# Expert activations turned by VectorE in blocks of 32x32 instead of by TensorE, in a one-layer SSD + GLA + MoE step

## The reference

```
def moe_ffn(h, comb, wg, wu, wd):
    out = jnp.zeros_like(h)
    for e in range(N_EXPERTS):                       # 16
        ye = (jax.nn.silu(h @ wg[e]) * (h @ wu[e])) @ wd[e]
        out = out + comb[:, e:e + 1].astype(h.dtype) * ye
    return out
```

## Time and profile before

| | before |
|---|---|
| median of 3 runs | 1048.48 us |
| profiled execution, its time | 1046.16 us |
| its span, first to last instruction | 1044.0 us |
| TensorE busy | 994.8 us (95%) |
| VectorE busy | 386.0 us (37%) |
| ScalarE busy | 232.8 us (22%) |
| read from memory, written | 212.31 MB, 24.36 MB |

### The profile page before, as it was taken

The page is one execution under the profiler, slowest core; times in us unless marked ns, Lnnn a source line. Parts: engine busy times, 40 slices in busy tenths (PEclk is TensorE's granted clock), DMA queues, the critical chain, the costliest instruction groups (busy, mean ns, idle before and its releaser), DMA issues.

```text
span 1044.0 us, 20310 instructions
## 1 busy us (share of the span) xinstructions
PE 994.8 (95%) x8547; PEld 750.8 (72%) x8547; DVE 386.0 (37%) x850; ACT 232.8 (22%) x466; POOL 138.0 (13%) x228
## 2 busy tenths in 40 slices
PE   4999999999989899999999999997889999999996
PEld 2667676676766566666666767665789999999981
DVE  3121235667435986656641611225110101101016
ACT  2131222323352222242251300002320101111013
POOL 0000232352000252422400000000100000000010
PEclk9999999999999899999999999999889999999998
DMA  9853346456453456655533633432739999999993
GB/s 381 317 197 121 122 161 207 157 211 220 148 195 119 177 184 214 219 208 196 175 140 121 251 121 121 161 106 82 291 140 349 408 406 405 392 398 412 391 355 122
DMA packets 47155, 237.62 MB, mean 228 GB/s; under 512 B 6800, under 2 KB 11248, under 8 KB 23792
## 3 DMA queue, kind: packets, MB, share of 16 engines
q1 hardware_dynamic: 45120, 230.85, 59.2%
q0 software_dynamic: 1520, 5.34, 1.5%
q10 hardware_dynamic: 448, 0.50, 0.1%
HBM read 212.31 MB, written 24.36 MB: 227 GB/s over the span
## 4 chain that ended last, share of the span: by engine, by line
PE 87%; DVE 4%; ACT 3%; issue 2%; DMA 1%; POOL 1%; ACTq 0%; DVEq 0%; SPq 0%; POOLq 0%
PE pjB L827 15%; PE pjA L827 14%; PE states L1370 11%; PE pjA L1218 7%; PE pjB L1218 7%; PE states L1373 6%; PE pjB L1370 3%; PE pjA L1370 3%; PE pjA L1373 1%; PE pjB L1373 1%; PE states L836 1%; PE bank L1182 1%; PE states L1197 1%; PE bank L951 1%; PE states L951 1%
## 5 line engine op out<-in xcount | busy, mean ns | idle before, releaser
L827 PE MATMUL pjB<-hF,ring 128*128 128x320 f32 x608 | 174.1, 440 | 0.0
L827 PE MATMUL pjA<-hF,ring 128*128 128x320 f32 x608 | 171.9, 436 | 0.5 <-ACT regA L1616 0.5
L1373 PE MATMUL states<-ring,oF 128*32 128x384 f32 x1392 | 155.3, 493 | 0.0
L1370 PE MATMUL states<-ring,oF 128*32 128x128 f32 x1392 | 155.3, 273 | 0.0
L1370 PEld LDWEIGHTS states<-ring,oF 128*32 128x32 f32 x1392 | 152.5, 110 | 0.6 <-issue 0.3
L827 PEld LDWEIGHTS pjB<-hF,ring 128*128 128x128 f32 x608 | 114.8, 192 | 49.7 <-issue 6.3
L827 PEld LDWEIGHTS pjA<-hF,ring 128*128 128x128 f32 x608 | 113.2, 190 | 50.7 <-issue 7.0
L2605 DVE TENSOR_TENSOR oF<-oF,states 128x384 f32<-128x384 f32 x15 | 8.3, 554 | 153.5 <-PE states L1373 153.5
L2337 DVE TENSOR_TENSOR G<-G 128x320 f32<-128x320 f32 x32 | 46.6, 1494 | 0.0
L1954 POOL TENSOR_TENSOR G<-regA,G 128x128 f32<-128x128 f32 (+1 forms) x32 | 18.9, 592 | 195.1 <-ACT G L1672 195.1
L1373 PE MATMUL pjB<-ring,hF 128*32 128x384 f32 x360 | 42.2, 493 | 0.0
(11 more groups left out here) (504 smaller groups left out, 1431.6 us busy)
## 6 DMA issues: line engine op xcount, KB each, us to landing
ring<-in_w SPq DMA_DIRECT2D x171, 1024.0 KB, 8.1
G<-in_ss SPq DMA_DIRECT2D x16, 512.0 KB, 4.0
out_ss_new<-G SPq DMA_DIRECT2D x16, 512.0 KB, 2.7
G<-csd SPq DMA_DIRECT2D x16, 320.0 KB, 3.5
G<-in_sg SPq DMA_DIRECT2D x4, 1024.0 KB, 6.2
out_sg_new<-G SPq DMA_DIRECT2D x16, 256.0 KB, 2.8
yd<-hF SPq DMA_DIRECT2D x14, 288.0 KB, 6.2
rF<-in_w SPq DMA_DIRECT2D x2, 1024.0 KB, 9.1
```

The costliest lines, as they stand in the source:

```text
L827: mm = pe.matmul(pj[g % 2][:, 0:T], w[:, k, half * P:half * P + P], hF[:, k, :], start=(k == 0), stop=(k == KT - 1))
L1370: pe.matmul(bank[CAP:P, c * P:(c + 1) * P], rows(c, True), w[:, WIDE:512], start=first and c == 0, stop=last, tile_position=(0, CAP), skip ...
L1373: mm = pe.matmul(bank[QUAD * c:QUAD * c + QUAD, 0:WIDE], rows(c, False), w[:, 0:WIDE], start=first, stop=last, tile_position=(0, QUAD * c) ...
```

## The change

All transposes but those of expert 15 leave TensorE. VectorE turns `actE` itself with 16 instructions per expert: each takes a block of 32 partitions (token block `c`) with three pieces of 32 columns, transposes the pieces, and writes them to partition group `q` of `actT`. The copy from bank 4 goes, except for expert 15 (`turned_last`). The wait for `s_rd` before `actE` is written again becomes a wait for `s_hev`, which VectorE's own last block counts.

```
             def down(e, back, turn=None):
...
                     mm.then_inc(s_used, 1)
-                    if turn and h == 0:
-                        turn_act(turn[0])
...
                     if isinstance(e, int) and e == 0:
                         for t in range(1, XROWS // P):
                             turn_tokens(t)
-                        turn_act(0)
...
                 def turned(e, v):
 
-                    dve.wait_ge(s_rd, GH + PAIRS + 1 + e)
+                    dve.wait_ge(s_eac, e + 1)
                     if not (isinstance(e, int) and e < 2):
                         moe_used(dve, e, 5, 2)
+                    for q in range(4):
+                        to = slice(QUAD * q, QUAD * q + QUAD)
+                        for c in range(4):
+                            at = slice(QUAD * c, QUAD * c + QUAD)
+                            rows = slice(QUAD * c, QUAD * c + QUAD) if c < BLOCKS else slice(CAP, P)
+                            ins = dve.transpose(actT[to, v, :, rows],
+                                                actE[at, :].rearrange("p (k f) -> p k f", f=P)[:, :, QUAD * q:QUAD * q + QUAD])
+                    ins.then_inc(s_hev, 1)
+
+                def turned_last(v):
+
+                    dve.wait_ge(s_rd, GH + PAIRS + 1)
+                    moe_used(dve, E - 1, 5, 2)
                     dve.tensor_copy(actT[:, v], b[4][:, 0:WIDE].rearrange("p (k c) -> p k c", k=BLOCKS)).then_inc(s_hev, 1)
```

In one() and last() the wait before `actE` changes in the same way:

```
-                        dve.wait_ge(s_rd, GH + PAIRS + e)
+                        dve.wait_ge(s_hev, XROWS // P + e)
```

More of the change, by code:

```diff
@@ L2617, in last @@
                     dve.wait_ge(s_esg, e + 1)
-                    dve.wait_ge(s_rd, GH + PAIRS + e)
+                    dve.wait_ge(s_hev, XROWS // P + e)
                     dve.tensor_tensor(actE, sgE, b[3][:, 0:WIDE], ALU.mult).then_inc(s_eac, 1)
-                    turned(e, v)
+                    turned_last(v)
                 def turned(e, v):
-                    dve.wait_ge(s_rd, GH + PAIRS + 1 + e)
+                    dve.wait_ge(s_eac, e + 1)
                     if not (isinstance(e, int) and e < 2):
                         moe_used(dve, e, 5, 2)
+                    for q in range(4):
[9 more added lines that the diff above has]
+                    moe_used(dve, E - 1, 5, 2)
                     dve.tensor_copy(actT[:, v], b[4][:, 0:WIDE].rearrange("p (k c) -> p k c", k=BLOCKS)).then_inc(s_hev, 1)
```

## The result

The changed kernel takes 1036.99 us (median of 4; 1031.66 to 1038.1) against 1047.87 for the kernel before (median of 4, the three above and one more): a ratio of 0.989 with a 95% interval of 0.985 to 0.993. A second series gave 1034.2 us (median of 6) against 1046.61 (median of 11), ratio 0.989 [0.987, 0.991]. It is faster by 11 to 12 us, about 1.1%. The forecast was 1047.5 with a range down to 1039, so it was wrong. The profiled execution took 1036.5 us, span 1034.4, before 1046.16 and 1044.0.

A forecast was written before the change was run, and what follows sets the result against it. Weight transfers at 400 GB/s, 16.7 us per expert, were taken as the bound close behind TensorE. 1.3 + 0.1 - 0.4 = 1.0 us off 1046.16 gave 1045.2, or 1047.5 on the median's scale (2.3 higher); range 1039 to 1051.

The forecast's parts named there:

- TensorE's part: Expert stage: fourteen sets of transposes at 0.83 us leave TensorE, 11.6 us less work.
- Expert 0's set: Transposes of expert 0, run at half clock: removing them was put at 0.3 to 0.6 us.
- What the weights allow: Weight loads in the expert stage: a 400 GB/s ceiling, 16.7 us per expert, leaves a gain of 1.0 us.
- The lead: Loads into the ring: landing grows 0.8 us per expert to 13.1 us, then TensorE waits for weights in each expert.
- Start gain: First load behind the transfer pause at expert 1 goes out earlier: 1.3 us gained.
- end lead: Fourth weight piece of expert 15 landed ahead of its use: 0.1 us of lead, added to the gain.
- store of expert 14: Results of expert 14 now stored before expert 15's last weights land: 0.4 us given back.
- Turning on VectorE: Sixteen VectorE transposes per expert at 0.26 us, 4.2 us in all, hidden and costing nothing.
- The cover of 0.5 us: Time left on VectorE between the end of turning and `y_half` becoming due, 4.8 against 5.26 us.
- the second rival: Slow turning makes TensorE wait at expert 14's down: 1054 us at the upper bound of 0.75 per instruction; chance 0.12.
- The point from which expert 14 pays: Expert 14's down loses nothing until turning passes 5.3 + 1.4 = 6.7 us after its start, 0.38 us per instruction.
- The first, TensorE stays the bound: Expert stage: transfers keep step at 425 GB/s, so the full 12 us are gained, 1036.5 us; chance 0.26.

The follow-up runs named there:

- e2: The kernel before the change with every set of three TensorE transposes issued four times: 1062.7 us.
- e7: e2 with both result stores of experts 0 to 13 cut to one row each: 1064.01 us.
- e3: The changed kernel with 2 of the 16 gate and up steps of each expert left out, all loads kept: 1026.39 us.
- e4: The changed kernel with 6 of the 24 steps of each expert left out, all loads kept: 1019.41 us.
- e1: The changed kernel with TensorE's transposes put back beside VectorE's turning: 1048.39 us, ratio 1.0007 to the kernel before.
- e12: e4 with both result stores of experts 0 to 13 cut to one row: 1012.0 us.

## Why the prediction was wrong

1. *TensorE's part.* Fourteen sets at 0.83 us, 11.6 us: right, 0.845 each over thirteen experts. That the real cost of a set is the gap in the sequence of steps and not its own row of 0.55 us held. Expert 0's set was put at 0.3 to 0.6 at the low clock; 0.35 was measured.
2. *What the weights allow: the step that failed.* The cost of the edit was right and the bound behind it was not. "Where a queue never empties, what is delivered is what can be delivered." From landing times that never fell to 5 us I took 400 GB/s, 16.7 us per expert, for the ceiling, and cut 12 us to 1. But 400 GB/s is simply what TensorE asked for: 6.68 MB in 16.56 us is 403. e2 shows the same standing landing time at 378 GB/s, e7 shows that the stores cause it, and e3 and e4 show what a full queue really delivers, 422. The two numbers agreed (16.7 and 16.56) because one was the cause of the other, not because two bounds met. The 0.14 us between them came from two landings only, 8.8 us at 800.0 and 9.9 at 982.4. Between these two the same load of the cycle (the one that goes out when down's last piece is used) landed in less:

```profile
L734 SPq DMA_DIRECT2D ring<-in_w x1: 333/333/333, 849.8 to 849.8; - x1
...
DMA to landing us min/median/max: 7.7/7.7/7.7
```

   A backlog in front of a ceiling does not shrink by 1.1 us in three experts while the demand stays.
3. *The lead.* Landing was to grow by 0.8 us per expert to 13.1. Once the stage had settled it grew from 9.9 us (the load issued at 833.6) to 10.7 (975.1), 0.1 us per expert, which is what 15.8 against 15.72 us gives. That is 1.4 us over fourteen experts, of a lead of about 4 (e3, e4).
4. *Start gain, end lead, store of expert 14* (1.3, 0.1 and 0.4 us): terms of a bound that did not exist. The lead of 0.1 us at the end was a reading of one execution. In e1, which has the same sets, loads and stores, the same load goes out at 1000.6 and lands in 9.3 us instead of 12.4, about 3 us ahead of its use; why it was late in the profile of the kernel before stays open. In the changed kernel it goes out at 988.2 and lands in 10.0 us, over 3 us ahead of its use.
5. *Turning on VectorE.* 16 x 0.26 = 4.2 us; 4.52 measured, the nearest row was right within 8%. The cover of 0.5 us was used up: `y_half` had no wait any more, one of the signs that I had named for the second rival. The point from which expert 14 pays was put 1.4 us too late, as it counted on the schedule of a bound by weights. So a little of this rival came true, 0.65 us.
6. *The rivals.* The first, TensorE stays the bound, is what happened, at its full price (1036.5 forecast, 1036.99 and 1034.2 measured). Its reason was another than the one I gave: nothing made the transfers faster, they had been able to do it before. It had a chance of 0.26, but its full price of 1036.5 lay below the range's lower end of 1039, so the range left out the very case it was to cover. What I held against it, that 427 GB/s was delivered by reads alone, was the nearest evidence and weighed too little: adding the stores' 0.39 MB at that rate gives 15.65 us. The Trainium skill's ceiling of 435 GB/s (DMA: Bandwidth & Descriptors, "Specifications") was the better guide than my reading of the queue; e4 reaches 422 of it. Every sign named for this rival came (the period to the end, over 420 GB/s), and none of those named for the forecast: no wait for a load, and no landing at 13 us.
7. *What would have shown it ahead of time.* The expert at 417 GB/s stood in the same table, and the landings of one load of the cycle, read in every expert, would have shown it too. A ceiling cannot be exceeded by 4% for a whole expert; a demand that follows stores unevenly can.

## What to carry to other kernels

A rate and a DMA share of 1.00 beside a busy engine do not tell a ceiling from a demand. In a steady loop the rate is bytes over period whoever sets the period (403 GB/s before, set by TensorE; 422 in e4, set by the transfers). If the busy engine's own steps fill the period, as the 24 steps and the transposes did, the transfers have shown nothing yet. In these runs a bound by transfers showed as waits that name a load and a landing time pinned at the depth of the ring; a long landing time came from stores in the same queue. When work moves from the bounding engine to one with slack, measure the slack up to the next consumer in its tightest place (here expert 14, 0.65 us short) and not in the steady loop alone.

## What the runs showed of the hardware

- The same loads at the same demand landed in 4.9 us without stores, 6.6 with stores from another engine's queue, and 9.5 with stores in their own queue, while the DMA share read 0.92 to 0.99. Why two stores of together 0.39 MB delay the loads of a whole expert stays open. At the ceiling they cost 1.0 us of period (e4 against e12), about their bytes.
- The DMA share does not measure the load here: 0.98 at 378 GB/s (e2), 1.01 at 402 (before) and 1.02 at 422 (e4).
- One wait of 4.77 us in the middle of dense work took TensorE's granted clock from 1.00 (980 to 985 us) to 0.50 (990 to 993), and the 8 steps behind it took 2.0 us more than at full clock.
- The same waits of TensorE near 760 us let the clock fall in one execution of the changed kernel (0.50) and not in another (1.00), 2.8 us apart.
- A VectorE transpose of 32 partitions x 96 float32, from one partition group into another, takes 0.27 us, 0.28 from start to start.
